# 32 unused bytes per partition ahead of the rounded activations: every later buffer starts half a 64-byte line further on

## The reference, cut to what matters

```
h = x
for layer in (0, 1):
    h = h + 0.5 * swiglu(rmsnorm(h), ffn_w_in, ffn_w_out)     # d_ff 2816
    h = h + mixer(rmsnorm(h))                                  # mlstm, then nsa
    h = h + 0.5 * swiglu(rmsnorm(h), ffn_w_in, ffn_w_out)
    (after layer 0: kv = shared K/V of nsa, with a compression MLP of 2048 -> 256 -> 64)
h = layer_norm(alpha * h + fox_mixer(h))
h = layer_norm(alpha * h + dsa_mixer(h))
```

## Time and profile before

| | |
|---|---|
| three runs | 1310.21, 1312.43, 1314.57 us |
| profiled execution, first to last instruction | 1310.3 us |
| mean granted TensorE clock | 0.992 |
| PE busy | 1270.2 us (97%), 6717 matmuls |
| PEld busy | 1077.6 us (82%) |
| DVE busy | 873.9 us (67%) |
| ACT busy | 613.6 us (47%) |
| DMA | 218.17 MB, mean 167 GB/s |

### The profile page before, as it was taken

One profiled execution on the slowest core, in us unless ns is written; L12 is line 12 of the kernel. 1 busy time (PEld: TensorE's weight loads), 2 busy tenths in 40 slices (PEclk: granted clock), 3 DMA queues, 4 the chain that ended last, 5 costly groups with the idle time before them and its releaser, 6 DMA issues.

```text
span 1310.3 us, 16491 instructions
## 1 busy us (share of the span) xinstructions
PE 1270.2 (97%) x6717; PEld 1077.6 (82%) x6717; DVE 873.9 (67%) x1312; ACT 613.6 (47%) x839; POOL 24.2 (2%) x37
## 2 busy tenths in 40 slices
PE   6999999989999999999999999999999999999997
PEld 5888888988788888878888886778888899988876
DVE  6655557885755556685657569856555567566896
ACT  6444346435434445444435357654444344544461
POOL 2000000100000000000000000000000000000000
PEclk9999999999999999999999989999999999999999
DMA  9655545443555556565665440065666686446401
GB/s 329 207 182 187 186 162 185 142 155 129 183 184 185 188 192 186 166 193 170 217 224 169 159 161 1 1 200 187 191 193 193 130 217 172 150 130 211 176 2 65
DMA packets 158812, 218.17 MB, mean 167 GB/s; under 512 B 8257, under 2 KB 110993, under 8 KB 158737
## 3 DMA queue, kind: packets, MB, share of 16 engines
q1 hardware_dynamic: 156880, 212.56, 51.2%
q0 software_dynamic: 1376, 3.71, 0.9%
q10 hardware_dynamic: 480, 0.85, 0.2%
HBM read 216.04 MB, written 1.05 MB: 166 GB/s over the span
## 4 chain that ended last, share of the span: by engine, by line
PE 82%; DVE 11%; issue 3%; ACT 2%; SPq 1%; DMA 1%; DVEq 0%
PE PS L686 23%; PE PS L689 23%; PE PS L687 23%; DVE wlo L2050 2%; PE PS L823 1%; PE PS L721 1%; PE PS L722 1%; ACT whi L1523 1%; PE PS L706 1%; PE PS L1300 1%; DVE arena L2639 1%; PE PS L728 1%; PE PS L1016 1%; SPq L591 1%; DVE XL L2090 1%
## 5 line engine op out<-in xcount | busy, mean ns | idle before, releaser
L2050 DVE TENSOR_TENSOR wlo<-raw,whi 128x2048 fp32r<-128x2048 f32 (+4 forms) x206 | 457.4, 2230 | 122.6 <-ACT whi L1523 121.8
L1523 ACT ACTIVATE whi<-raw 128x2048 fp32r<-128x2048 f32 (+4 forms) x206 | 381.4, 1863 | 63.4 <-DMA raw<-in_fox_w_in_dram 33.1
L686 PE MATMUL PS<-whi,XL 128*128 128x512 f32 (+3 forms) x992 | 385.8, 390 | 8.9 <-DVE scr L2152 3.8
L687 PE MATMUL PS<-wlo,XH 128*128 128x512 f32 (+3 forms) x992 | 379.8, 384 | 0.0
L689 PE MATMUL PS<-whi,XH 128*128 128x512 f32 (+3 forms) x992 | 265.0, 384 | 0.0
L686 PEld LDWEIGHTS PS<-whi,XL 128*128 128x128 f32 x992 | 187.3, 189 | 45.1 <-DVE scr L2152 4.9
L689 PEld LDWEIGHTS PS<-whi,XH 128*128 128x128 f32 x992 | 185.5, 190 | 35.5
L687 PEld LDWEIGHTS PS<-wlo,XH 128*128 128x128 f32 x992 | 187.4, 189 | 32.9
L1577 ACT ACTIVATE scr<-PS,rn 128x256 f32<-128x256 f32 x88 | 41.7, 474 | 225.2 <-PE PS L689 223.9
L686 PE MATMUL PS<-whi,GL 128*128 128x512 f32 x320 | 125.4, 392 | 0.0
L687 PE MATMUL PS<-wlo,GH 128*128 128x512 f32 x320 | 124.6, 389 | 0.0
(11 more groups left out here) (387 smaller groups left out, 1339.2 us busy)
## 6 DMA issues: line engine op xcount, KB each, us to landing
raw<-in_ffn_w_in_dram SPq DMA_DIRECT2D x174, 512.0 KB, 5.0
raw<-in_ffn_w_out_dram SPq DMA_DIRECT2D x88, 512.0 KB, 4.9
raw<-in_fox_w_in_dram SPq DMA_DIRECT2D x24, 512.0 KB, 7.9
raw<-in_a_w_in_dram SPq DMA_DIRECT2D x16, 512.0 KB, 4.6
raw<-in_dsa_w_in_dram SPq DMA_DIRECT2D x16, 512.0 KB, 6.0
raw<-in_kv_w_dram SPq DMA_DIRECT2D x12, 512.0 KB, 4.2
raw<-in_fox_w_in_dram SPq DMA_DIRECT2D x12, 344.0 KB, 5.0
raw<-in_a_w_out_dram SPq DMA_DIRECT2D x8, 512.0 KB, 4.9
```

Source lines behind the costliest of these rows:

```text
L686: mm(o, xl, wh, start=start and i == 0, stop=False, skip_group_check=True)
L687: mm(o, xh, wl, start=False, stop=False, skip_group_check=True)
L1523: A(whi[:, p % SLOTS, 0:n], raw[:, p % SLOTS, 0:n], ACT.Copy).then_inc(hi_done, 1)
L2050: V.tensor_tensor(wlo[:, p % SLOTS, 0:n], raw[:, p % SLOTS, 0:n], whi[:, p % SLOTS, 0:n].bitcast(F32), ALU.subtract).then_inc(lo_done, 1)
```

## The change

More of the change, by code:

```diff
@@ L155, in program @@
         h = sb("h", [P, NT, D])
+        sb("half_line", [P, 8])
         XH = sb("XH", [P, KT, T], F32R)
```

## The result

The changed kernel takes 1332.59 us (median of 4 runs, 1330.75 to 1333.22); the kernel before, run beside it, 1313.33 us (4 runs, 1310.21 to 1314.57). The ratio is 1.0151, 95% interval [1.0135, 1.0167]: the change makes it about 1.5%, 19 us, slower.

A forecast was written before the change was run, and what follows sets the result against it. PE was taken to bound the kernel, with 82% of the chain of waits. Terms -12.2 + 0.3 + 0.3 = -11.6 us took 1312.4 to 1300.8 us; own range 1294 to 1309, with the rivals 1294 to 1333.

The forecast's parts named there:

- the first term: 4080 matmuls with stationary XH, XL, GH, GL and 512 or 384 moving columns: -3.3 ns each, -12.2 us at the end.
- the 90%: Share of the PE time of L686, L687 and L689 on the chain of waits: 904 of 1007 us, scaling gains.
- Kind B: 960 matmuls of 256 columns where XH and XL are the moving operand: +0.3 ns each, +0.3 us.
- The lower bound of -3.3 ns: Cheapest price for the 256-column matmuls with moving XH, XL, if only the offset between the two operands counts.
- `FH` and `FL`: 96 matmuls of the compression whose stationary operand moves onto a line: from 116.7 to 120.0 ns, +0.3 us.
- ACT, DVE, weights, other widths: Engine work, weight DMAs into raw, and the few matmuls of 344, 372, 272 and 48 columns: all costed at nothing.
- the forecast's own range: 1294 to 1309 us for the whole kernel: both gains in full, or 60% of the main gain with 256-column matmuls dearest.
- The rival of the unsettled rhythm: 512-column matmuls never settle after transposes, staying near 232.0 ns: +5.3 ns each, +18.0 us, 1331 us; chance 0.34.
- The rival without effect: Addresses don't matter to PE: 1312.4 us unchanged, or 1316.7 with only the moving-XH, XL matmuls dearer; chance 0.20.

The follow-up runs named there:

- e8: Kernel before with buffers and a pad moved ahead: XH and XL start 224 bytes, GH and GL 352 bytes off the weights' start; 1332.32 us, ratio 1.0153.
- e13: Kernel before, but every third 512-column product (high by high) loads only 64 of 128 stationary columns; 1321.16 us, ratio 1.0074.
- e2: The change with a pad of 64 bytes in place of its 32, against the kernel before; 1332.24 us, ratio 1.0158.
- e9: Kernel before with ss and rv (256 bytes together) ahead of XH, so XH, XL, xs, GH, GL, scr and con are at offset 256; 1311.29 us, ratio 1.0002.
- e1: Kernel before with the 32-byte pad ahead of everything, weight buffers too; 1311.82 us, ratio 1.0004.
- e11: Kernel before with views into larger buffers: XH and XL at offset 16, GH and GL at 8 from the weights' start; 1324.04 us, ratio 1.0085.
- e12: Kernel before with XH and XL at offset 160, GH and GL at 240 from the weights' start; 1326.91 us, ratio 1.0107.
- e15: Kernel before with views of XH and XL 16 bytes further on in the stage with most 256-column matmuls, offset 0 elsewhere; 1310.32 us, ratio 0.9988.

## Why the prediction was wrong

**The step that failed** is the price of the first term: "I take the difference seen at 256 columns, -3.3 ns, since the 13.3 ns over the columns were the same at 512 and at 256". The right price is +5.6 ns for X and +6.2 for G. The equality at offset 0 said nothing about other offsets. e8 puts 512-column matmuls at the very offset at which `FH` gave 116.7, 224, and they run at 233.15; the reading of `FH` was right and its transfer to another width was not. The term came to -13.6 us, -12.2 with the 90%, and is +23.1 (16.5 + 6.6). Nor was -3.3 ns a fixed price at its own width and offset: in e13, where `FH` and `FL` start as in the kernel before, 47 of these matmuls take 117.7 ns each and not 116.7.

**The assumption under it** was also wrong: that the unit is the 64-byte line and that "half a line in" is one state. e2 costs as much as the change, and e9 shows the unit to be 256 bytes. So `FH` before (224) and `XH` after (32) were never at the same offset. The addresses in the source showed that the two places differ, though not that it matters.

**Kind B** was +0.3 us and is -2.7. The nearest row that I took, 344 columns with mixed starts, hides the effect, since that width hardly depends on the offset (157.3 and 157.6 ns). The lower bound of -3.3 ns, "if only the offset between the two operands counts", was the right reading. In the compression of the kernel before the moving operand starts 32 bytes further on (modulo 256) than the stationary one, and so it does in kind B after the change: 116.7 ns there, 116.8 in the stretch here. A second such pair agrees as well, `FH` in e2 (118.4) and kind B in e8 (118.3), with 224 between moving and stationary operand.

**`FH` and `FL`** were +0.3 us and are +0.3, 116.7 to 119.65 ns. It was a size read from kind B at the offset to which they moved, at the same width, and that transfer held. In part this was luck: the row was chosen because both start on a line, and e2 shows that this is not enough.

**ACT, DVE, weights, other widths, the share of the chain.** The zeros held: busy times within 0.4 us, 384 columns within 0.2 ns. The factor of 90% was about right: the medians differ by 19.3 us, 93% of the sum of 20.7, and in the other kernels with a loss it is 80 to 99%. Two ends of the forecast's own range don't follow from its terms to the digit, which give 1295.6 us with both gains in full and 1309.7 on the other side; nothing hangs on it.

**The rival of the unsettled rhythm** is what happened: 1331 us against 1332.59, +5.3 ns against +5.6 and +6.2, at the point that it named, with an alternation, though between 232 and 235 ns and not 224 and 236. That the mean of a transient is so near the lasting one is not explained, and its total is close in part by luck: kind B was at +0.3 us and is at -2.7. I gave it 0.34 and not more because its row showed a transient. But it was a row of the width concerned, and the row of my forecast wasn't. Within the rival one thing was off: it also put the step at the 64-byte line, and at the stationary operand's own start, which e1 excludes.

**The rival without effect** falls with the result. From the Trainium skill's "SBUF — State Buffer", which has a read port for each operand (section "SBUF: two separate sides") and 16-byte lines (section "Specifications (TRN2)"), the prediction inferred that 32 bytes change nothing. The page does not say so itself. The 226.7 and 233.3 ns at two offsets contradict the inference, though not the description of ports and lines, which no run here shows.

**What stays open** is the mechanism. The runs show that the offset modulo 256 bytes sets which paces occur, that the fastest one at 512 columns is lost when one load in three is half as long, and that one shifted operand of three slows its neighbours. They don't show what inside the chip has this period, why 512 columns lose where 256 gain and 384 mostly stay (173.3 to 176.7), nor what the 13.3 ns are. In the changed kernel, e11, e12 and e15 one offset gives two paces in different stretches; what chooses between them wasn't tried.

## What to carry to other kernels

Where weights are reloaded for every matmul and most matmuls move 512 columns, let the stationary and the moving buffer start at the same place modulo 256 bytes in the partition, and look again after any buffer ahead of one of them changes its size: 32 bytes cost 1.5% here with every count, wait and engine load unchanged. Read the pace from the distance between starts over a dozen matmuls, not from their records, of which the 512-column ones grew by 4 to 6 ns while the distance grew by 6. And carry a price over only between matmuls of one width and one offset, and even then look at more than one stretch; where a row of the right width and one of the right address disagree, neither is proof. Here the row of the right width was the better guide, though it came from an unsettled stretch.

## What the runs showed of the hardware that was not expected

- The pace of a stream of 512-column matmuls depends on the relative start of its operands with a period of 256 bytes: 226.7 ns settled at 0, and averages of 230.7 at 8, 232.1 at 16, 233.2 at 32, 233.3 at 64, 234.1 at 96, 232.7 at 128, 233.3 at 160, 229.15 at 192, 233.2 at 224, 228.1 at 240. At 16 and 240 the average mixes stretches of 226.7 with slower ones, 233.3 at 16. The average at 0, unsettled stretches included, is 227.1 to 227.5.
- Even 8 bytes count (230.7), less than any line that I had considered.
- At 256 columns the order is nearly turned around: 119.9 at 0 and 96, 119.0 at 128, 117.0 at 32, 115.6 at 16, and 113.3 for stretches of e15. At 32 there are stretches of 116.8 and of 120.0 in one execution.
- Halving the weight load of one matmul in three, 188 to 134 ns, slows the stream from 226.7 to about 230 ns.
